# A fused decoder layer: three expert weight sets loaded before the experts start, and routing done tile by tile inside the output projection

## The reference

```python
x = x + (sigmoid(gate_a) * A + sigmoid(gate_b) * B) @ w_out      # merge, output projection, residual
h = rms_norm(x, norm2)                                            # rows scaled by 1/rms, then by the gain
logits = h @ [w_route_group | w_route_expert] + b                 # 4 group logits, 32 expert logits
group = argmax(first 4);  two best of the 8 experts in that group
y = x + sum over the two: weight * (silu(h @ w_gate[e]) * (h @ w_up[e])) @ w_down[e]
```

## Time and profile before

| | us |
|---|---|
| median of 3 runs | 1594.57 |
| lowest and highest run | 1590.17, 1601.40 |
| the profiled execution's own time | 1597.39 |
| its span, first to last instruction | 1595.8 |
| mean granted TensorE clock | 0.887 of full speed |

### The profile page before, as it was taken

How to read it: one execution, slowest core, us unless ns; L and a number is a source line. 1 busy time by engine, 2 the same in 40 slices (tenths; PEclk the granted TensorE clock), 3 DMA queues, 4 the chain that set the end, 5 groups by cost and what they waited for, 6 DMA issues and landing times. The chain is left out here.

```text
span 1595.8 us, 26066 instructions
## 1 busy us (share of the span) xinstructions
PE 1260.4 (79%) x10498; PEld 774.4 (49%) x10498; DVE 495.6 (31%) x1016; ACT 263.6 (17%) x537; POOL 191.9 (12%) x238
## 2 busy tenths in 40 slices
PE   5999969989994585677356999839888878887983
PEld 3885557779992464433124874513333333332331
DVE  2002346726646362664441211241111101111113
ACT  2000143202220122453000001201111101111110
POOL 0000111200000540243211000001111110111100
PEclk9999989889998697798677999859999989999996
DMA  7013112250001863432726841249999999999984
GB/s 312 17 53 121 42 49 74 81 126 4 4 4 59 246 192 80 126 101 119 213 81 243 306 172 52 110 177 354 399 405 406 410 407 410 404 415 403 413 373 178
DMA packets 89081, 324.86 MB, mean 204 GB/s; under 512 B 25257, under 2 KB 57178, under 8 KB 74282
## 3 DMA queue, kind: packets, MB, share of 16 engines
q1 hardware_dynamic: 69018, 291.80, 47.8%
q0 software_dynamic: 11184, 25.17, 4.9%
q10 hardware_dynamic: 8768, 6.29, 1.4%
HBM read 306.36 MB, written 28.92 MB: 210 GB/s over the span
## 5 line engine op out<-in xcount | busy, mean ns | idle before, releaser
L2512 DVE TENSOR_TENSOR e_g<-e_g,PS 64x512 f32<-64x512 f32 x32 | 22.1, 690 | 323.5 <-ACT e_g L2477 323.5
L289 PE MATMUL PS<-scr,p_w 128*128 128x272 f32 (+2 forms) x448 | 105.7, 399 | 6.1 <-DVE scr L356 6.1
L2419 PE MATMUL PS<-first,e_xs 128*64 128x512 f32 x352 | 90.8, 675 | 22.5 <-DMA first<-in_w_exp_up 21.8
L892 PE MATMUL PS<-scr 128*128 128x272 f32 x384 | 93.8, 409 | 12.8 <-PEq L2564 12.8
L2419 PE MATMUL PS<-second,e_xs 128*64 128x512 f32 x352 | 84.3, 634 | 17.0 <-DMA second<-in_w_exp_up 16.3
L289 PEld LDWEIGHTS PS<-scr,p_w 128*128 128x128 f32 (+2 forms) x448 | 84.0, 188 | 27.4 <-issue 6.9
L2419 PE MATMUL PS<-e_w,e_xs 128*64 128x512 f32 x320 | 78.3, 646 | 23.6 <-DMA e_w<-in_w_exp_up 23.6
L892 PEld LDWEIGHTS PS<-scr 128*128 128x128 f32 x384 | 76.1, 199 | 29.6 <-issue 13.1
L2361 POOL DMA_INDIRECT xe<-scratch_h_dram,toks x32 | 29.9, 936 | 382.4 <-PE PS L2409 277.5
L2060 PE MATMUL PS<-m_oT,xe 128*128 128x272 f32 x256 | 65.4, 415 | 13.2 <-DMA m_oT<-scratch_oa_dram 11.4
L301 PE MATMUL PS<-p_w,scr 128*128 128x512 f32 (+1 forms) x192 | 70.7, 529 | 0.0
(11 more groups left out here) (539 smaller groups left out, 1984.7 us busy)
## 6 DMA issues: line engine op xcount, KB each, us to landing
first<-in_w_exp_gate SPq DMA_DIRECT2D x11, 2048.0 KB, 12.8
first<-in_w_exp_up SPq DMA_DIRECT2D x11, 2048.0 KB, 17.3
first<-in_w_exp_down SPq DMA_DIRECT2D x11, 2048.0 KB, 23.3
second<-in_w_exp_gate SPq DMA_DIRECT2D x11, 2048.0 KB, 27.7
second<-in_w_exp_up SPq DMA_DIRECT2D x11, 2048.0 KB, 32.1
second<-in_w_exp_down SPq DMA_DIRECT2D x11, 2048.0 KB, 23.8
e_w<-in_w_exp_gate SPq DMA_DIRECT2D x10, 2048.0 KB, 28.6
e_w<-in_w_exp_up SPq DMA_DIRECT2D x10, 2048.0 KB, 33.0
```

Of the source, the lines that this page charges most:

```text
L289: last = nc.tensor.matmul(out[:, n], w[:, s % NW, c, a:a + m], hT[:, c, n * TH:n * TH + TH], start=(c == 0), stop=(c == KC - 1))
L892: last = M(gate_ps(u)[:, n], wgate[:, u % 2, c, :], hT[:, c, n * TH:n * TH + TH], start=(c == 0), stop=(c == KC - 1))
L2419: last = M(ps, xs[:, b, c, :], w[s][m][:, c * DE:c * DE + DE], start=(c == 0), stop=(c == KC - 1))
L2512: V.tensor_tensor(g[:, b, :], g[:, b, :], psU, ALU.mult).then_inc(h_out, 1)
```

## The change

- The two stages become one (`tail`), with the weight semaphores `w_in` shared, so a load can be issued in one block and awaited in the other, and no clearing of semaphores or barrier of a stage stands between them. Each block still ends by joining the engines.
- One buffer `big` holds `hT`, `oT` and `mT` and afterwards a set of expert weights. The sets are now `first`, `big`, `second` for experts 0, 1, 2. Gate and up of expert 1 are loaded after the last merge product; down of expert 1 and up of expert 2 after the last projection. Gate and down of expert 2 are issued in `experts` when expert 0's rows have arrived.
- The sample rows are projected first. Each tile is handled in halves: DVE adds a half to the residual and multiplies it by the gain into `h2` (now in `second[0]`); PE transposes the unscaled `x1`, ACT copies it out; the gain is folded into the routing weights once (during the merge), and 1/rms is applied to the logits and, by ACT, to `h2`.
- Group, experts, rank and table of a tile are made while PE projects the next tile. Tables are made for the 32 experts only.
- The rest of the routing (overflow tables, weights of the two experts) moves into `experts`, behind experts 3 to 6 on DVE, with small matmuls behind experts 3 and 5 on PE.
- The last `h2` store is issued by ACT instead of SP.

```diff
                 sp.wait_ge(gates_mm, 2 * KC)
-                sp.dma_start(second[0][:], expert_matrix(io, 0, 1)).then_inc(first_in, 16)
-                for i in range(5):
-                    sp.wait_ge(h2_ready, i + 1)
...
+                for m in range(2):
+                    sp.dma_start(X[m], expert_matrix(io, m, 1)).then_inc(w_in[1][m], 16)
+                for p in range(4):
+                    i = order[p]
+                    sp.wait_ge(h2_ready, p + 1)
...
                 sp.wait_ge(out_mm, 9)
-                for m in (1, 2):
-                    sp.dma_start(second[m][:], expert_matrix(io, m, 1)).then_inc(first_in, 16)
-                sp.wait_ge(first_stored, 16)
+                sp.dma_start(X[2], expert_matrix(io, 2, 1)).then_inc(w_in[1][2], 16)
+                sp.dma_start(second[1][:], expert_matrix(io, 1, 2)).then_inc(w_in[2][1], 16)
                 sp.wait_ge(h2_stored, 16 * 4)
-                sp.wait_ge(first_in, 16 * 6)
...
+                for q in (2, 3, 4):
+                    i = order[q]
+                    project(i, 0, range(0, 2))
+                    turn(q - 1, 1)
+                    project(i, 0, range(2, 4))
+                    logits(q - 1)
+                    if q == 2:
+                        table(0)
+                    project(i, 0, range(4, 8))
+                    project(i, 1, range(0, 4))
+                    rank(q - 1)
+                    project(i, 1, range(4, 6))
+                    turn(q, 0)
+                    project(i, 1, range(6, 8))
+                    table(q - 1)
+                turn(4, 1)
+                logits(4)
+                rank(4)
+                table(4)
...
+                    V.tensor_tensor(xs, xs, PS[:, 512 * (n % 2):512 * (n % 2) + 512], ALU.add).then_inc(x1_ready, 1)
...
+                    V.tensor_tensor(h2[:, p % 4, cols], xs, n2[:, cols], ALU.mult).then_inc(xn_ready, 1)
...
+                for q in (2, 3, 4):
+                    stats(q - 1)
+                    choose(q - 1)
+                    half(q, 0)
+                    place(q - 1)
+                    half(q, 1)
+                stats(4)
+                choose(4)
+                place(4)
...
+                act.dma_start(io["h2_dram"][3 * P:4 * P, :], h2[:, 0]).then_inc(h2_stored, 16)
...
-                for n in range(2, NE):
+                sp.wait_ge(x_in[0], 16)
+                for m in (0, 2):
+                    sp.dma_start(w[2][m], expert_matrix(io, m, 2)).then_inc(w_in[2][m], 16)
+                for n in range(NS, NE):
...
+                    if n == 3:
+                        counts()
+                    if n == 4:
+                        one_hots()
+                    if n == 5:
+                        overflow_tables()
+                    if n == 6:
+                        weights()
...
-            stage(merge_and_route, cst, wk, x1, first, second, xe, slots, toks, ids)
-            stage(experts, cst, wk, x1, first, second, xe, slots, toks, ids)
+            stage(tail, cst, wk, x1, first, big, second, xe, slots, toks, ids, late)
```

More of the change, by code:

```diff
@@ L104 @@
 NCST = CONST_AT["headrow"][0]
+NLATE_HELD = 80
+NLATE = sum(CONST_AT[k][1] for k in LATE_CONSTS)
 PAR_AT = {}
@@ new lines, in turn @@
+                def turn(p, h):
+                    i = order[p]
+                    pe.wait_ge(x1_ready, 2 * p + h if p else 1)
+                    if p:
+                        pe.wait_ge(turn_out, 2 * (p - 1) + h + 1)
+                    for c in range(4 * h, 4 * h + 4):
+                        last = nc.tensor.transpose(PS[:, 2048 + c * P:2048 + c * P + rows[i]],
+                                                   x1[0:rows[i], i, c * P:c * P + P], cst["ident"][0:rows[i], 0:rows[i]])
+                    last.then_inc(turn_mm, 1)
@@ new lines, in rank, with table @@
+                def rank(p):
+                    pe.wait_ge(oh_ready, p + 1)
+                    last = M(PS[:, 1024:1024 + NE], cst["before"], ohs[:], start=True, stop=(p == 0))
+                    if p:
+                        last = M(PS[:, 1024:1024 + NE], cst["ones"], cum[:, p - 1], start=False, stop=True)
+                    last.then_inc(rank_mm, 1)
+                def table(p):
+                    pe.wait_ge(hot_ready, p + 1)
+                    for k in range(2):
+                        last = M(PS[0:CAP, 1536:1536 + NE], is_row[:, k], hot[:, k], start=(p == 0 and k == 0), stop=(p == 4 and k == 1))
+                    last.then_inc(table_mm, 1)
@@ new lines, in scale @@
+                def scale(p):
+                    r = rows[order[p]]
+                    act.wait_ge(rstd_ready, p + 1)
+                    act.wait_ge(xn_ready, 2 * p + 2)
+                    A(h2[0:r, p % 4], h2[0:r, p % 4], ACT.Copy, scale=ss[0:r, p:p + 1]).then_inc(h2_ready, 1)
+                square(0, 0)
+                square(0, 1)
+                root(0)
+                turned(0, 0)
+                turned(0, 1)
+                scale(0)
+                turned(1, 0)
+                square(1, 0)
@@ new lines, in _ @@
+                samples()
+                stats(0)
+                half(1, 0)
+                choose(0)
+                half(1, 1)
+                place(0)
+                for q in (2, 3, 4):
[7 more added lines that the diff above has]
+                place(4)
+                link(V.tensor_copy(tot[:], cum[:, 4]))
@@ L2276, in expert_matrix, with experts @@
     return src[bass.ds(e, 1)].rearrange("a (p c) n -> p (a c n)", p=P)
-def experts(nc, io, PS, sem, cst, wk, x1, first, second, xe_all, slots, toks, ids):
+def experts(nc, io, PS, sem, cst, wk, x1, first, big, second, xe_all, slots, toks, ids, late, w_in):
     with ExitStack() as ctx:
@@ L2288, in experts @@
         NS = 3
-        w = [first, second, [t(f"e_w2_{m}", [P, 2 * HW]) for m in range(3)]]
+        w = [[m[:] for m in first], expert_set(big), [m[:] for m in second]]
         NX = 3
@@ L2548, in _, with tail @@
                         dve.wait_ge(added, 2 * p + k + 1)
+def tail(nc, io, PS, sem, cst, wk, x1, first, big, second, xe, slots, toks, ids, late):
+    w_in = [[sem(f"w_in{s}_{m}") for m in range(3)] for s in range(3)]
+    merge_and_route(nc, io, PS, sem, cst, wk, x1, first, big, second, xe, slots, toks, late, w_in)
+    experts(nc, io, PS, sem, cst, wk, x1, first, big, second, xe, slots, toks, ids, late, w_in)
 def build(nc, io):
```

458 lines of the change are left out of this document (256 added, 202 removed).

## The result

The changed kernel takes 1571.04 us (median of 4 runs, 1570.28 to 1575.78) beside 1592.94 us for the kernel before in the same measurement: ratio 0.986, 95% interval 0.983 to 0.9889. The forecast was 1575. The profiled execution has a span of 1569.2 us, 26.6 less than before.

A forecast was written before the change was run, and what follows sets the result against it. The expert-weight load stream was taken as the bound, its end hanging on expert 0's down. Rows arriving 21.4 us earlier gave 1576.0 from the profiled 1597.4, 1573.2 against the median; forecast 1575 us, range 1566 to 1588.

The forecast's parts named there:

- Step 1: PE in the output projection: projection, samples, transposes, logits, ranks and table sum to 75 us, ending at 1030.1.
- E: The moment the last projection ends on PE, forecast at 1030.1 against 1021.7 for the same work before.
- Step 2: Routing of four of five tiles hides under projection: DVE 8.5 us per tile under PE's 17; costed at nothing.
- an uncovered routing: Rival, 4%: in the projection, four tiles' 8.5 us of DVE routing run in the open, 34 us later: 1610.
- the clock: Rival, 3%: finer-cut projection drops TensorE to 1.2 GHz, its 128 records cost 55 us more: 1631.
- Step 3: Routing tail behind the last projection: the table of rows, `toks`, is ready at E + 9.9.
- Step 4: Last `h2` store: issued at E + 5.3, takes 7 us beside two loads, lands at E + 12.3, ends the block.
- Steps 5 and 6: Border to the gather's issue 1.6 us; gather alone 3.0 us; rows arrive at 1047.0, 21.4 us earlier.
- Step 7: Gain folding in the merge, moved expert 2 loads, routing behind experts 3 to 6, ACT's table load: cost nothing.
- the extra matrix in the merge by itself is worth nothing: Loading seven matrices in the merge gains nothing: paid back by one load fewer at the border, 11 either way.
- more is gained: Rival, 7%: below 1568, if table and store both finish early and the projection's start runs warm.
- The tail's rival: Rival, 20%: store or gather near their upper rows, or stalls at PE's piece borders; gain 8 to 16 us, 1581 to 1589.

The follow-up runs named there:

- before_wait: The kernel before, with SP waiting for expert 0's rows before it issues expert 2's three loads; 1592.89 us, ratio 1.0004.
- routing_twice: Second run of the changed kernel's routing with the loads placed as in the kernel before; 1573.94 us beside 1570.76 for the unaltered changed kernel.
- down_earlier: The changed kernel with expert 2's down matrix also issued after the last projection, one matrix more ahead; 1574.34 us, ratio 0.989.
- routing_only: First run of the changed kernel's routing with the loads placed as in the kernel before; 1578.55 us, ratio 0.991.
- up_later: The changed kernel with expert 2's up matrix issued only when expert 0's rows have arrived, one matrix fewer ahead; 1570.25 us, ratio 0.9866.

## Why the prediction was right, step by step

- **The whole.** From expert 1's gate issue to the end it was 642.6 us before and 619.3 to 620.3 in three profiles after: 22.3 to 23.3 us, forecast 21.4. In three measurements the timed medians of the changed kernel lay 20.8 to 23.6 us below those of the kernel before. Of the profiles' distance some 3 us are the two slow-clock stretches of the one profile before; the forecast had carried the first of them over into its own sum (29.43 in step 1), so like for like it is 19 to 20 against 21.4. The mechanism held, and that the number is closer than this is luck.
- **Step 1 (E, 75.0 us behind the stage's start).** It was 72.0 (950.87 to 1022.85). Adding up the distances from each row of PE to the next: projection 56.5 (forecast 57.3), logits 5.9 (6.8), transposes 3.7 (4.0), ranks and table 2.3 (3.1), samples 3.6 (3.7). The small records were mostly overpriced: the samples' logits were priced as a whole tile's and took 0.64. The projection ran at a granted clock of 1.00 from the start (0.94 before); by the rows of `before_wait`, also at 1.00, its 128 records cost 55.6 in whole tiles, so the new piece borders took 0.9 and the clock gave back 1.7.
- **Step 2 (routing hidden).** Held: PE is busy for 29.13 us of 29.13 and 42.85 of 42.85 in the projection's windows. The rivals of an uncovered routing and of the clock fall with that row.
- **Step 3 (`toks` at E + 9.9).** E + 10.0 (1032.88).
- **Step 4 (store lands at E + 12.3).** The term that was mis-sized: issued at E + 4.8 (forecast 5.3), but landing in 10.8 us and not 7, so E + 15.6. That the store and not the table lets go the block was right. The runs show the store landing about when the second load does (in the changed kernel at 1038.5 and 1038.3), or the only one (5.2 us), and no later beside three.
- **Steps 5 and 6.** Border 1.2 (forecast 1.6), gather 2.9 (3.0). From the stage's start to the rows 91.7 us, forecast 91.9: steps 1 and 4 were off by 3.0 and 3.3 in opposite directions, and much of the close hit is that.
- **Step 7 (edits at nothing).** Held. From the load behind expert 0's down the loads behind those of experts 1 to 3 follow every 12.42 us, as before. With the moved routing, expert 4's comes some 0.5 later than before (50.2 against 49.7) and expert 6's 1.0 (83.1 against 82.1), but expert 7's 1.7 earlier (101.7 against 103.4). Over 440 us from 1074.74 the transfers have a share of 1.01 at 409 GB/s, as in the earlier trace rows.
- **Where the argument was wrong: "the extra matrix in the merge by itself is worth nothing".** `routing_twice` shows about 3 us. The reason given, that it is paid back at the border, leaves out that loads still due at the border must also have landed by the time down ends; without the early matrix they have not (the load behind down lands in 11.8 us and not 8.0). `down_earlier` shows that a further matrix is in fact worth nothing.
- **The rival "more is gained"** named a warm start of the projection; that happened, though it is not the change's doing (`before_wait` has it with the old code, and two profiles of the new code have not), and the store took back what E gained. The tail's rival had the right place (store and loads meet) and too high a price.

The 22 to 23 us between the profiles are then some 16 from the routing under the projection, its smaller tables and the shorter border (no run takes these apart), some 3 from the matrix that loads while the transfers are idle, and some 3 from the clock in the profile of the kernel before. The 16 is what `routing_only` and `routing_twice` leave of that profile's distance (19.4 and 19.5) without the clock's part; in their timed runs they lie 14.7 and 20.4 us below the kernel before.

## What to carry to other kernels

Where a stream of loads sets the end, look for each stretch in which it stands still and ask what ends it: a buffer that comes free, or bytes not yet loaded; a step that removes one stops paying where the other begins, so 5 us won for the rows by `up_later` came back as nothing. A small transfer on the critical path is delayed by the loads issued beside it, but holding the loads back cost the stream most or all of what the small transfer gained. Measure changes of a few us in the profile from the nearest unaltered event, since the work ahead of it scattered by up to 13 us, and compare the same products at both ends of the stretch, since a lower granted clock there added up to 3 us.

## What the runs showed that was not expected

- A 512 KB store lands in 2.6 us alone, 5.1 to 5.2 beside one 2 MiB load, 10.2 to 11.7 beside two, 10.8 beside three; the step from two to three cost nothing in the one profile that has it.
- While PE waits for expert 0's rows, its granted clock is 0.50 (the 1.2 GHz level); it is still 0.50 in 1042.88 to 1046.88 and 0.62 in the next 4 us, and the first 32 products of expert 0 take 9.74 us against 7.04 for the same work of expert 2:

```profile
1055.98 7.09 PE L2501 MATMUL PS<-big,e_xs 128*64 128x512 f32 x32 [0.69 <-ACT e_xs L2562]
...
1068.45 7.04 PE L2501 MATMUL PS<-second,e_xs 128*64 128x512 f32 x32
```

  These 2.7 us lie on the way to the load behind down; before it was 9.19 us.
